# Running the F and B threads of a macro-step beside E, C, D and A, with x and h staged in one buffer each

## The chip, the cores and the metric

The kernel runs on all 8 cores of one Trainium2 chip. Each core computes one sequence of the batch and exchanges nothing with the others. The metric is the device time of the slowest core, in microseconds.

## The reference

One layer of a streaming encoder, for each sequence of 8192 frames of 1024 features:

```python
h = layer_norm(x, ln_in_g, ln_in_b)
q, k, v, g_ret, x_lru, g_lru, m_ret, m_lru = split(h @ w_in)      # 512 512 1024 1024 1024 1024 1024 1024
ret = chunk_retention(rotary(q), rotary(k), v)                    # 4 heads, 64-frame chunks, carried state
ret = head_group_norm(ret)
ret_branch = (silu(g_ret) * ret) @ w_ret_proj
hl = rg_lru(causal_depthwise_conv(x_lru))                         # gates by 8 blocks of 128x128, linear recurrence
lru_branch = (silu(g_lru) * hl) @ w_lru_proj
merged = sigmoid(m_ret + b0) * ret_branch + sigmoid(m_lru + b1) * lru_branch
h = layer_norm(2 ** 0.25 * h + merged @ w_out, ln_out_g, ln_out_b)
```

## The kernel before

**Tiling.** The 8192 frames are done in 16 macro-steps of 512 frames (TM), each in four pieces (s) of 128 frames. Weights are held in DRAM as 20 units of 128 x 4096 in bfloat16 (1 MB each; in macro-step 0 they are loaded as float32 in eight pieces of 256 KB and cast on ScalarE on the way) and go through a ring of four slots in SBUF.

**Threads.** The work of a macro-step m is written as six Python generators. Each yields after a small piece, and what it has recorded up to then goes to the in-order queues of the engines:
- A(m): for each piece, load x (512 KB), statistics, normalize (VectorE), store h to DRAM (`hscr`, issued by GpSimd), eight fp32 transposes into hT. 24 yields.
- B(m): units 0 to 3. Units 0 and 1 give q and k, with rotary on VectorE and GpSimd through the single buffers rA and rB; units 2 and 3 give v, copied by ScalarE. One PSUM bank a piece and unit. 44 yields.
- C(m): retention for two pairs of heads. For each, four recurrence steps (9 yields), then four gate groups of unit 4 or 5 (eight matmuls, four transposes, tanh, multiply; 4 yields). 104 yields.
- D(m): the gated recurrence, units 6 to 9, two channel groups in lockstep: front (two times 16 matmuls, convolution, gates) and back (root, scan, product). 13 steps a pair, 52 yields.
- E(m): units 10 to 17, for each two gates and two projections (32 matmuls) and their merge into mrg. 48 yields.
- F(m): units 18 and 19, for each piece load h from `hscr`, 16 matmuls, sum, statistics, normalize, store the output (issued by GpSimd). 16 yields.

**Order.** `interleave` takes turns: in a round each thread advances by its weight. A macro-step is two stages: first B(m+1) at weight 2 and F(m-1) at weight 1, then E(m), C(m+1) at weight 2, D(m+1) and A(m+2). There is no barrier between stages; the queues of the engines run in the order recorded. Which of the eight PSUM banks a thread may use is given by its BankPool.

**Ring.** `use(m, u)` takes a resident unit, `done(m, u)` gives its slot back and issues, on SyncE's (SP's) queue, the next unit in order of first use. All loads (units, x, h, rot) are issued by SP in the order recorded, and SP waits in that order for a tile to be free.

**Staging.** `xs` is `obuf`, two tiles of 128 x 1024: A loads x into it two pieces ahead, and F builds its output in it. `hA`, one tile, takes A's normalized h, from which it is stored and transposed, and in F the h loaded from `hscr`. A tile may be written again when its readers, a store's landing among them, are done.

## Time and profile before

| | us |
|---|---|
| median of 3 runs | 4004.73 |
| lowest and highest | 4000.53, 4128.72 |
| the profiled execution | 4020.5 |
| its slowest core (core 6), span | 4019.0 |
| its fastest core (core 3), span | 3991.4 |

The profile shows one execution, on its slowest core. TensorE's granted clock is 0.861 of full speed on that core as a mean, and 0.875 on core 3. A span runs from the first to the last instruction. Busy times of TensorE come from modelled ends, since its matmuls are pipelined.

### The profile page before, as it was taken

Reading aid. Unit: us, or ns where it says so; the run is one execution under the profiler, and the core shown is the slowest. Engines: PE = TensorE matmul, PEld = TensorE weight load, DVE = VectorE, ACT = ScalarE, POOL = GpSimd, SP = SyncE. Lnnn points to the kernel's source line nnn. Section 1 sums busy time; section 2 is a strip of 40 time slices with the busy share of each in tenths; the row PEclk is TensorE's granted clock in tenths of the full one; section 3 lists DMA queues with packets and bytes.
Section 4 is the critical chain, followed back from the end, with each engine's and each line's share of the span. In section 5 each row is a group of like instructions: output and inputs, shape, how many; then the busy total and the mean of one; then the engine's idle time right before and its main releaser. Section 6 shows DMA issues by size and latency. Waiting matters only on the chain.

```text
span 4019.0 us, 47416 instructions; the slowest of 8 cores (3991.4 to 4019.0 us)
## 1 busy us (share of the span) xinstructions
PE 2956.7 (74%) x13056; PEld 1342.7 (33%) x13056; DVE 2192.0 (55%) x3601; ACT 1608.8 (40%) x2530; POOL 1541.2 (38%) x2121
## 2 busy tenths in 40 slices
PE   0446555878787877778787877778787787878786
PEld 0222222333333333333333333333333333333332
DVE  1154333655565575665666565556656565566454
ACT  2254445242534435343434434343443534343440
POOL 0133222434353443444443443435334344434332
PEclk9766667989898998889898998889898888988888
DMA  6432433524333342424334242424334252433323
GB/s 183 143 120 81 147 118 118 181 98 168 103 133 131 108 173 87 162 105 160 111 111 156 105 163 105 170 95 145 120 114 167 89 176 95 164 116 112 122 100 142
DMA packets 109987, 522.51 MB, mean 130 GB/s; under 512 B 12448, under 2 KB 12576, under 8 KB 68768
## 3 DMA queue, kind: packets, MB, share of 16 engines
q1 hardware_dynamic: 88416, 431.38, 31.6%
q0 software_dynamic: 18432, 67.12, 4.1%
q10 hardware_dynamic: 2880, 20.97, 1.3%
q8 instruction: 111, 1.82, 0.2%
q14 instruction: 148, 1.21, 0.1%
HBM read 431.35 MB, written 88.08 MB: 129 GB/s over the span
## 4 chain that ended last, share of the span: by engine, by line
PE 38%; DVE 21%; issue 12%; ACT 10%; DMA 9%; POOL 9%; DVEq 1%; ACTq 0%; SPq 0%; POOLq 0%
PE pb L180 36%; DMA wst<-wpack 6%; DVE xc L162 5%; PE pb L184 2%; ACT ta L154 2%; DVE obuf L162 2%; POOL rA L158 2%; DVE gst L573 2%; POOL grs L158 2%; DVE S L162 1%; ACT ring L176 1%; DVE hA L162 1%; DMA obuf<-x 1%; POOL kdec L158 1%; DVE Sb L172 1%
## 5 line engine op out<-in xcount | busy, mean ns | idle before, releaser
L180 PE MATMUL pb<-hT,ring 128*128 128x512 bf16 x5120 | 1351.1, 420 | 108.0 <-DVE rA L162 87.2
L180 PEld LDWEIGHTS pb<-hT,ring 128*128 128x128 bf16 x5120 | 538.7, 106 | 774.9 <-issue 360.3
L180 PE MATMUL pb<-ring,hT 128*128 128x512 bf16 x2048 | 535.5, 420 | 158.3 <-DVE rB L158 125.1
L158 POOL TENSOR_TENSOR retT<-rB,rA 128x512 bf16<-128x512 f32 x128 | 204.7, 1600 | 489.9 <-DVE rA L162 462.5
L180 PEld LDWEIGHTS pb<-ring,hT 128*128 128x128 bf16 x2048 | 211.3, 105 | 467.1 <-issue 293.0
L154 ACT ACTIVATE xhat<-pb,gnm,grs 128x256 f32<-128x256 f32 x256 | 130.7, 561 | 585.5 <-POOL gnm L167 576.7
L180 PE MATMUL pb<-xcb,rgw_sb 128*128 128x512 bf16 x256 | 127.7, 505 | 278.7 <-DVE xcb L172 119.1
L180 PE MATMUL pb<-retT,ring 128*128 128x512 bf16 x1024 | 281.2, 424 | 63.5 <-ACT tr L154 63.1
L162 DVE SCALAR_TENSOR_TENSOR xc<-xl,vecs_sb,xc 128x512 f32<-128x512 f32 x384 | 292.0, 774 | 27.3 <-ACT xl L176 0.2
L184 PE MATMUL pb<-identf,hA 128*128 128x128 f32 x512 | 95.9, 321 | 277.5 <-DVE hA L162 150.4
L176 ACT CAST qkr<-rA 128x512 bf16<-128x512 f32 x64 | 39.6, 618 | 594.3 <-POOL rA L158 592.4
L180 PE MATMUL pb<-lruT,ring 128*128 128x512 bf16 x1024 | 243.3, 381 | 25.9 <-ACT tl L154 25.7
L672 DVE TENSOR_TENSOR_SCAN ti<-av,carry,ta 128x512 f32<-128x512 f32 x128 | 249.9, 1991 | 7.2 <-POOL ta L158 7.2
L162 DVE SCALAR_TENSOR_TENSOR rA<-rA,pb 128x512 f32<-128x512 f32 x128 | 87.8, 686 | 284.9 <-ACT rA L154 281.7
L167 POOL TENSOR_SCALAR lrs<-lmv 128x1 f32<-128x1 f32 x128 | 43.2, 338 | 518.3 <-DVE lmv L452 448.2
L180 PE MATMUL pb<-ring,mrg 128*128 128x512 bf16 x1024 | 232.7, 381 | 2.9 <-DVE rA L162 1.1
L158 POOL TENSOR_TENSOR grs<-gmv,small_sb 128x2 f32<-128x2 f32 x128 | 26.2, 204 | 514.3 <-DVE gmv L575 472.1
L158 POOL TENSOR_TENSOR mrg<-tr,tl 128x512 bf16<-128x512 f32 x128 | 163.0, 1274 | 156.2 <-DVE tl L162 154.4
L450 DVE BATCH_NORM_STATS2 lst<-obuf 128x6 f32<-128x512 f32 x64 | 44.2, 690 | 314.6 <-DMA obuf<-x 314.4
L158 DVE TENSOR_TENSOR rA<-pb,rot_sb 128x512 f32<-128x512 f32 x128 | 88.5, 692 | 210.1 <-POOL qkr L158 71.8
L154 ACT ACTIVATE rA<-pb 128x512 f32<-128x512 f32 x128 | 76.1, 595 | 309.2 <-PE pb L180 263.8
L176 ACT CAST ring<-wst 128x512 bf16<-128x512 f32 x160 | 98.8, 617 | 249.8 <-DMA wst<-wpack 202.0
(84 smaller groups left out, 5024.9 us busy)
## 6 DMA issues: line engine op xcount, KB each, us to landing
ring<-wscr SPq DMA_DIRECT2D x300, 1024.0 KB, 5.5
wst<-wpack SPq DMA_DIRECT2D x160, 256.0 KB, 3.3
obuf<-x SPq DMA_DIRECT2D x64, 512.0 KB, 5.3
hscr<-hA POOLq DMA_DIRECT2D x64, 512.0 KB, 3.5
hA<-hscr SPq DMA_DIRECT2D x64, 512.0 KB, 4.2
out<-obuf POOLq DMA_DIRECT2D x64, 512.0 KB, 3.5
wscr<-ring ACTq DMA_DIRECT2D x20, 1024.0 KB, 6.0
rot_sb<-rot SPq DMA_DIRECT2D x16, 256.0 KB, 5.8
```

The costliest lines, as they stand in the source:

```text
L154: return lambda e: e.activation(out, in_, func, **kw)
L158: return lambda e: e.tensor_tensor(out, a, b, op)
L162: return lambda e: e.scalar_tensor_tensor(out, a, sc, b, op0, op1)
L167: return lambda e: e.tensor_scalar(out, a, s1, None, op0)
L172: return lambda e: e.tensor_copy(out, in_)
L176: return lambda e: e.copy(out, in_)
L180: return lambda e: e.matmul(out, lhsT, rhs, start=start, stop=stop)
L184: return lambda e: e.transpose(out, in_, ident)
L450: S.op("dve", lambda e, xt=xt: e.bn_stats(lst[:, 0:6], xt[:, 0:512]), reads=[xk], writes=["lst0"])
L573: S.op("dve", lambda e, hl=hl, bO=bO: e.bn_stats(gs_[:, hl * 6:(hl + 1) * 6], pb[bO][:, hl * 256:(hl + 1) * 256]), reads=[PK(bO)], writes= ...
L672: S.op("dve", lambda e, c=c, di=di: e.tensor_tensor_scan(ti[di][:], av[di][:], ta[di][:], carry[:, c:c + 1], ALU.mult, ALU.add), reads=[(" ...
```

## The change

The two stages become one. In each macro-step four threads are interleaved: F(m-1) followed by E(m) (weight 1, banks 6 and 7 for both); B(m+1) followed by C(m+1) (weight 2, banks 0 and 1); D(m+1) (weight 1, banks 2 to 4); A(m+2) (weight 1, bank 5). B had banks 4 to 7 and F banks 0 to 3.

The staging becomes two tiles with one use each. `xs[0]` takes x, is normalized in place, and is stored and transposed from there. `hland[0]` takes h in F, and the sum, the normalization and the output store work in it. `load_x(m, s)` now stands right ahead of the statistics of its piece, and `load_h(m, s)` at the top of each piece of F. One tile of 128 x 1024 less is used.

```diff
--- before.py
+++ after.py
@@ -287,10 +287,8 @@
         mhalf = T("mhalf", [128, 8], F32)
         rgw = T("rgw_sb", [128, 2, 8, 128], BF16)
         ring = [T("ring%d" % i, [128, 4096], BF16) for i in range(RING)]
-        obuf = [T("obuf%d" % i, [128, D], F32) for i in range(2)]
-        xs = obuf
-        hA = [T("hA%d" % i, [128, D], F32) for i in range(1)]
-        hland = hA
+        xs = [T("xs0", [128, D], F32)]
+        hland = [T("hland0", [128, D], F32)]
         wst = [T("wst%d" % i, [128, 512], F32) for i in range(2)]
         hT = [T("hT%d" % i, [128, 8, TM], BF16) for i in range(3)]
         rot = T("rot_sb", [128, NS * 128], F32)
@@ -391,9 +389,9 @@
             S.dma("sp", "c_small", small[:], small_d, writes=["small"])
             S.dma("sp", "c_vecs", vecs[:].rearrange("p a b -> p (a b)"), vecs_d, writes=["vecs"])
             rgflat = rgw[:].rearrange("p a b c -> p (a b c)")
-            for hf in range(2):
-                S.dma("sp", "c_rgw%d" % hf, obuf[hf][:], rgw_d[:, hf * 1024:(hf + 1) * 1024], writes=[("obuf", hf)])
-                S.op("dve", f_copy(rgflat[:, hf * 1024:(hf + 1) * 1024], obuf[hf][:]), reads=[("obuf", hf)], writes=["rgw"])
+            for hf, (stg, stk) in enumerate(((xs[0], ("xs", 0)), (hland[0], ("hl", 0)))):
+                S.dma("sp", "c_rgw%d" % hf, stg[:], rgw_d[:, hf * 1024:(hf + 1) * 1024], writes=[stk])
+                S.op("dve", f_copy(rgflat[:, hf * 1024:(hf + 1) * 1024], stg[:]), reads=[stk], writes=["rgw"])
             S.op("dve", f_copy(identb[:], identf[:]), reads=["identf"], writes=["identb"])
             S.op("pool", f_memset(mhalf[:], -0.5), writes=["mhalf"])
             S.op("pool", f_memset(S32[:], 0.0), writes=[("S32", h) for h in range(4)])
@@ -424,12 +422,12 @@
                 if m >= n_macro:
                     return
                 t0 = m * TM + s * 128
-                S.dma("sp", "xl%d" % (s % 2), xs[s % 2][:], x_d[t0:t0 + 128, :], writes=[("obuf", s % 2)])
+                S.dma("sp", "xl0", xs[0][:], x_d[t0:t0 + 128, :], writes=[("xs", 0)])
 
             def load_h(m, s):
                 t0 = m * TM + s * 128
                 S.dma("sp", "hl0", hland[0][:], hscr_d[t0:t0 + 128, :],
-                      reads=[("hscr", m, s)], writes=[("hA", 0)])
+                      reads=[("hscr", m, s)], writes=[("hl", 0)])
 
 
             def hTk(m, s, half):
@@ -440,35 +438,30 @@
 
             def Athread(m, pool):
                 hTm = hT[m % 3]
-                load_x(m, 0)
-                load_x(m, 1)
+                xk = ("xs", 0)
+                xt = xs[0]
                 for s in range(NS):
-                    xk = ("obuf", s % 2)
-                    xt = xs[s % 2]
-                    hk = ("hA", 0)
-                    hb = hA[0]
-                    S.op("dve", lambda e, xt=xt: e.bn_stats(lst[:, 0:6], xt[:, 0:512]), reads=[xk], writes=["lst0"])
-                    S.op("dve", lambda e, xt=xt: e.bn_stats(lst[:, 6:12], xt[:, 512:1024]), reads=[xk], writes=["lst1"])
+                    load_x(m, s)
+                    S.op("dve", lambda e: e.bn_stats(lst[:, 0:6], xt[:, 0:512]), reads=[xk], writes=["lst0"])
+                    S.op("dve", lambda e: e.bn_stats(lst[:, 6:12], xt[:, 512:1024]), reads=[xk], writes=["lst1"])
                     S.op("dve", lambda e: e.bn_aggr(lmv[:], lst[:]), reads=["lst0", "lst1"], writes=["lmv"])
                     yield
                     S.op("pool", f_ts(lrs[:], lmv[:, 1:2], LN_EPS, None, ALU.add), reads=["lmv"], writes=["lrs"])
                     S.op("pool", f_tt(lrs[:], lrs[:], mhalf[:, 0:1], ALU.pow), reads=["lrs", "mhalf"], writes=["lrs"])
                     yield
-                    S.op("dve", f_stt(hb[:], xt[:], lmv[:, 0:1], lnig[:], ALU.subtract, ALU.mult),
-                         reads=[xk, "lmv", "lnig"], writes=[hk])
-                    S.op("dve", f_stt(hb[:], hb[:], lrs[:], lnib[:], ALU.mult, ALU.add),
-                         reads=[hk, "lrs", "lnib"], writes=[hk])
-                    if s + 2 < NS:
-                        load_x(m, s + 2)
+                    S.op("dve", f_stt(xt[:], xt[:], lmv[:, 0:1], lnig[:], ALU.subtract, ALU.mult),
+                         reads=[xk, "lmv", "lnig"], writes=[xk])
+                    S.op("dve", f_stt(xt[:], xt[:], lrs[:], lnib[:], ALU.mult, ALU.add),
+                         reads=[xk, "lrs", "lnib"], writes=[xk])
                     t0 = m * TM + s * 128
-                    S.dma("pool", "hs0", hscr_d[t0:t0 + 128, :], hb[:], reads=[hk], writes=[("hscr", m, s)])
+                    S.dma("pool", "hs0", hscr_d[t0:t0 + 128, :], xt[:], reads=[xk], writes=[("hscr", m, s)])
                     yield
                     for half in range(2):
                         b = pool.get()
                         for j in range(4):
                             kc = half * 4 + j
-                            S.op("pe", f_tr(pb[b][:, j * 128:(j + 1) * 128], hb[:, kc * 128:(kc + 1) * 128], identf[:]),
-                                 reads=[hk, "identf"], writes=[PK(b)], inc=(j == 3))
+                            S.op("pe", f_tr(pb[b][:, j * 128:(j + 1) * 128], xt[:, kc * 128:(kc + 1) * 128], identf[:]),
+                                 reads=[xk, "identf"], writes=[PK(b)], inc=(j == 3))
                         yield
                         src = pb[b][:].rearrange("p (k t) -> p k t", k=4)
                         dst = hTm[:, half * 4:half * 4 + 4, s * 128:(s + 1) * 128]
@@ -716,12 +709,10 @@
                     yield
 
             def Fthread(m, pool):
-                load_h(m, 0)
+                ob = hland[0]
+                ok = ("hl", 0)
                 for s in range(NS):
-                    ob = obuf[s % 2]
-                    ok = ("obuf", s % 2)
-                    hl = hland[0]
-                    hlk = ("hA", 0)
+                    load_h(m, s)
                     bY = [pool.get(), pool.get()]
                     for hf in range(2):
                         slot = use(m, 18 + hf)
@@ -733,13 +724,11 @@
                         done(m, 19)
                     yield
                     for hf in range(2):
-                        S.op("dve", f_stt(ob[:, hf * 512:(hf + 1) * 512], hl[:, hf * 512:(hf + 1) * 512], 2.0 * ALPHA,
+                        S.op("dve", f_stt(ob[:, hf * 512:(hf + 1) * 512], ob[:, hf * 512:(hf + 1) * 512], 2.0 * ALPHA,
                                           pb[bY[hf]][:], ALU.mult, ALU.add),
-                             reads=[hlk, PK(bY[hf])], writes=[ok])
-                    if s + 1 < NS:
-                        load_h(m, s + 1)
-                    S.op("dve", lambda e, ob=ob: e.bn_stats(lst2[:, 0:6], ob[:, 0:512]), reads=[ok], writes=["lst20"])
-                    S.op("dve", lambda e, ob=ob: e.bn_stats(lst2[:, 6:12], ob[:, 512:1024]), reads=[ok], writes=["lst21"])
+                             reads=[ok, PK(bY[hf])], writes=[ok])
+                    S.op("dve", lambda e: e.bn_stats(lst2[:, 0:6], ob[:, 0:512]), reads=[ok], writes=["lst20"])
+                    S.op("dve", lambda e: e.bn_stats(lst2[:, 6:12], ob[:, 512:1024]), reads=[ok], writes=["lst21"])
                     S.op("dve", lambda e: e.bn_aggr(lmv2[:], lst2[:]), reads=["lst20", "lst21"], writes=["lmv2"])
                     yield
                     S.op("pool", f_ts(lrs2[:], lmv2[:, 1:2], 4.0 * LN_EPS, None, ALU.add), reads=["lmv2"], writes=["lrs2"])
@@ -748,7 +737,7 @@
                     S.op("dve", f_stt(ob[:], ob[:], lmv2[:, 0:1], lnog[:], ALU.subtract, ALU.mult), reads=[ok, "lmv2", "lnog"], writes=[ok])
                     S.op("dve", f_stt(ob[:], ob[:], lrs2[:], lnob[:], ALU.mult, ALU.add), reads=[ok, "lrs2", "lnob"], writes=[ok])
                     t0 = m * TM + s * 128
-                    S.dma("pool", "os%d" % (s % 2), out_d[t0:t0 + 128, :], ob[:], reads=[ok])
+                    S.dma("pool", "os0", out_d[t0:t0 + 128, :], ob[:], reads=[ok])
                     yield
 
             def chain(*gs):
@@ -762,22 +751,21 @@
                 th.append((Athread(1, BankPool(S, [5])), 1))
             interleave(th)
             for m in range(n_macro):
-                th = []
+                p3 = BankPool(S, [6, 7])
+                g3 = [Ethread(m, p3)]
+                if m >= 1:
+                    g3.insert(0, Fthread(m - 1, p3))
+                th = [(chain(*g3), 1)]
                 if m + 1 < n_macro:
-                    th.append((Bthread(m + 1, BankPool(S, [4, 5, 6, 7])), 2))
-                if m >= 1:
-                    th.append((Fthread(m - 1, BankPool(S, [0, 1, 2, 3])), 1))
-                interleave(th)
-                th = [(Ethread(m, BankPool(S, [6, 7])), 1)]
-                if m + 1 < n_macro:
-                    th.append((Cthread(m + 1, BankPool(S, [0, 1])), 2))
+                    p1 = BankPool(S, [0, 1])
+                    th.append((chain(Bthread(m + 1, p1), Cthread(m + 1, p1)), 2))
                     th.append((Dthread(m + 1, BankPool(S, [2, 3, 4])), 1))
                 if m + 2 < n_macro:
                     th.append((Athread(m + 2, BankPool(S, [5])), 1))
                 interleave(th)
             run_gen(Fthread(n_macro - 1, BankPool(S, [0, 1, 2, 3])))
-            S.wait_all("pool", [("obuf", 0), ("obuf", 1)] + [("hscr", n_macro - 1, s) for s in range(NS)])
-            S.wait_all("sp", [("ring", i) for i in range(RING)] + [("hA", 0), "rot"])
+            S.wait_all("pool", [("hl", 0), ("xs", 0)] + [("hscr", n_macro - 1, s) for s in range(NS)])
+            S.wait_all("sp", [("ring", i) for i in range(RING)] + [("hl", 0), ("xs", 0), "rot"])
             S.wait_all("act", [("ring", i) for i in range(RING)] + [("wscr", u) for u in range(NU)])
 
         record = []
```

## Rows read from the trace of the kernel before

**Rows 1.** The page: busy time, share of the span, instructions, by engine
```profile
PE 2956.7 (74%) x13056; PEld 1342.7 (33%) x13056; DVE 2192.0 (55%) x3601; ACT 1608.8 (40%) x2530; POOL 1541.2 (38%) x2121
```

**Rows 2.** Windows: length, busy of each engine (PE, PEld, DVE, ACT, POOL), clock, DMA
```profile
1616.40:1672.60 56.20, 47.59 (x206) 20.39 (x205) 33.89 (x54) 7.78 (x14) 29.42 (x39) 0.90 0.55 195
1672.60:1717.00 44.40, 33.85 (x164) 16.40 (x162) 29.94 (x50) 21.86 (x34) 14.63 (x22) 0.85 0.48 162
1717.00:1770.40 53.40, 41.12 (x188) 19.10 (x186) 30.76 (x47) 25.29 (x40) 25.08 (x35) 0.87 0.26 96
1770.40:1809.30 38.90, 30.73 (x147) 14.01 (x145) 23.65 (x45) 18.91 (x29) 12.87 (x20) 0.87 0.24 86
1809.30:1844.50 35.20, 27.75 (x128) 13.13 (x125) 18.82 (x30) 20.59 (x32) 13.62 (x19) 0.92 0.26 90
1832.20:1844.50 12.30, 7.84 (x37) 4.19 (x36) 6.66 (x7) 8.99 (x13) 9.20 (x7) 0.92 0.27 85
3895.00:3968.00 73.00, 61.31 (x264) 26.84 (x263) 31.22 (x42) 9.63 (x14) 20.75 (x23) 0.89 0.48 173
3968.00:4019.00 51.00, 27.32 (x126) 11.97 (x123) 24.50 (x33) 2.75 (x4) 13.58 (x15) 0.81 0.28 103
```

**Rows 3.** Timeline of TensorE: start, length, instructions, idle before and releaser
```profile
1627.13 3.62 PE L180 MATMUL pb<-ring,mrg 128*128 128x512 bf16 x16
...
1630.59 3.62 PE L180 MATMUL pb<-ring,hT 128*128 128x512 bf16 x16
...
1659.11 11.66 PE L180 MATMUL pb<-ring,hT 128*128 128x512 bf16 x40 [3.38 <-DVE rB L158]
...
1841.34 2.53 PE L180 MATMUL pb<-hT,ring 128*128 128x512 bf16 x8 [2.72 <-DVE rA L162]
```

**Rows 4.** Timeline of GpSimd, at the end of the B/F stage
```profile
1655.60 1.84 POOL L158 TENSOR_TENSOR kdec<-rA,small_sb 128x512 bf16<-128x512 f32 x1
...
1665.87 0.65 POOL L108 DMA_DIRECT2D out<-obuf  x1 [1.96 <-DVE obuf L162]
```

**Rows 5.** Timeline of VectorE, the macro-step from 1616 us and the last F
```profile
1623.00 0.69 DVE L158 TENSOR_TENSOR rA<-pb,rot_sb 128x512 f32<-128x512 f32 x1 [5.61 <-DMA rot_sb<-rot]
1623.61 0.74 DVE L158 TENSOR_TENSOR rB<-pb,rot_sb 128x256 f32<-128x256 f32 x2
...
1658.88 1.48 DVE L162 SCALAR_TENSOR_TENSOR obuf<-hA,pb 128x512 f32<-128x512 f32 x2
...
1662.18 1.31 DVE L162 SCALAR_TENSOR_TENSOR obuf<-obuf,lmv,lnog 128x1024 f32<-128x1024 f32 x1
...
1678.48 0.69 DVE L450 BATCH_NORM_STATS2 lst<-obuf 128x6 f32<-128x512 f32 x1 [13.17 <-DMA obuf<-x]
...
1680.97 4.84 DVE L162 SCALAR_TENSOR_TENSOR xc<-xl,vecs_sb,xc 128x512 f32<-128x512 f32 x6
...
1711.36 4.61 DVE L672 TENSOR_TENSOR_SCAN ti<-av,carry,ta 128x512 f32<-128x512 f32 x2 [0.28 <-POOL ta L158]
...
3984.09 0.69 DVE L162 SCALAR_TENSOR_TENSOR obuf<-hA,pb 128x512 f32<-128x512 f32 x1 [2.10 <-PE pb L180]
...
4006.77 1.48 DVE L162 SCALAR_TENSOR_TENSOR obuf<-hA,pb 128x512 f32<-128x512 f32 x2
```

**Rows 6.** The page's DMA issues: count, size of one, us to landing
```profile
wst<-wpack SPq DMA_DIRECT2D x160, 256.0 KB, 3.3
...
hA<-hscr SPq DMA_DIRECT2D x64, 512.0 KB, 4.2
...
out<-obuf POOLq DMA_DIRECT2D x64, 512.0 KB, 3.5
```

**Rows 7.** Timeline of SyncE's DMA queue
```profile
1616.24 0.37 SPq L108 DMA_DIRECT2D rot_sb<-rot  x1
...
1671.33 0.81 SPq L108 DMA_DIRECT2D obuf<-x  x2
```

**Rows 8.** DMA issues of the stretch from 1640 to 1652 us
```profile
ring<-wscr SPq DMA_DIRECT2D x3, 1024.0 KB, 8.7
```

## Prediction

> **What bounds the kernel now.** I read the busy times first [rows 1]: TensorE is busy 74% of the span, VectorE 55%, nothing else over 40%. No engine is full, so the time is set by waits between engines, and a sum over engines says little. Next I looked for the period. The windows are cut where TensorE starts the first matmuls of a D unit pair or of a B stage [rows 2]: 56.2 + 44.4 + 53.4 + 38.9 + 35.2 = 228.1 us is one steady macro-step. The first window is the separate stage of B and F, the other four are the 13-round quarters of the stage of E, C, D and A. The B/F stage is already TensorE's densest (47.6 of 56.2 us); the quarters are busy 76, 77, 79 and 79%. So the stage that the change dissolves is not the one with the holes. Its own hole is B's rotary on the single rA/rB buffers: TensorE waits 3.4 us for VectorE [rows 3], which waits for GpSimd's rA and kdec work of 1.84 us [rows 4]. At its end VectorE idles 13.2 us for x [rows 5], while TensorE has forty matmuls to do, most of them of v (11.7 us, [rows 3]): that wait costs little now.
>
> **The new order, counted in rounds.** A round is one turn of the interleave. By their yields B has 44 steps at two a round (22 rounds), C 104 (52), D 52, A 24, F 16, E 48. Before, a macro-step had 22 + 52 rounds. After, F then E takes rounds 0 to 63, B then C 0 to 73, D 0 to 51, A 0 to 23. The number of rounds is 74 both times; what changes is what shares a round. Matmuls of 512 columns run at 0.216 us each at full clock (16 in 3.46 us, [rows 3]), and their number doesn't change. So the question is how long each stretch takes.
>
> **Rounds 0 to 16.** I walked the emission order with the durations of the rows. TensorE has in it 64 matmuls of F, 88 of B, 68 of D, 8 of E, and 20 transposes: about 52 us. VectorE has four F pieces at 5.7 us (two sums and the statistics from 1658.88 to about 1662, two normalizing steps of 1.3), eight rotary pieces at 1.35 (0.61 to the start of the second row, and its 0.74), three A pieces at 4.3 (statistics 1.6, normalizing 2.6), and of D two convolutions of 4.84 us, scans of 3.8 (up to 4.6) and ten smaller ones at about 0.7 (an estimate by the 0.69 of the other 128x512 rows): 67 us [rows 5]. VectorE, not TensorE, is thus the longer one here, where it was the shorter one in both stages before (33.9 of 56.2 and 29.9 of 44.4, [rows 2]). Onto it come three waits that the single buffers bring:
> - F. h, the sum and the output now share one tile. load_h(s+1) must wait until the output store has landed, then land itself. A store lands 3.5 us after its issue, a load of h takes 4.2 [rows 6], with issue about 9 us from the last multiply to the next sum; VectorE has 3 to 6 us of other work in between. Cost: 5.6 us before piece 1, 3.4 before piece 2.
> - A. The load of x stands right ahead of its statistics. For piece 1 it comes a little after h(1) and is covered. For piece 2, in round 12, it stands in SP's queue behind load_h(3) and behind three ring units (2, 10 and 3), because F has just given back two slots and B one. A 256 KB load behind one ring unit took 6.7 us (issued 1616.24, VectorE released 1623.00, [rows 5, 7]); the middle one of three ring units landed after 8.7 us [rows 8]. Three units ahead of x make some 10 us more than the 4.2 of h: 14 us, and it is VectorE that stands.
> - SP and the ring. F holds two of four slots to round 12. Unit 2, wanted in round 14, is issued behind load_h(3), that is behind the landing of out(2); TensorE waits some 10 us there, beside VectorE's wait for x and not on top of it.
> F's matmuls also have two banks instead of four and stand behind A's transposes, which wait for VectorE. The walk ends at: round 3 at 20 us, round 5 at 32, round 9 at 53, round 12 at 64, round 13 at 82, round 16 at 92 us. From below: without any DMA wait it is VectorE's 67 us plus 8 to start, 75. From above: each F piece at its full 15 us when nothing overlaps, plus the x wait, plus D's convolution behind it, 100. I take the walk's **92**.
>
> **Rounds 17 to 73.** Rounds 17 to 25 hold 100 matmuls and smalls, 25 us of TensorE work; at the 77% of the second quarter [rows 2] that is 32. Rounds 26 to 38 hold what the third quarter holds: 39. Rounds 39 to 51: like the fourth, or the second without A, so between 35.2 and 38.9: 37. Rounds 52 to 63 have E and C's recurrence without D: 18 us of TensorE work, and the third quarter scaled to 12 rounds gives 36 as the upper bound; C's serial steps fill much of it, 26. Rounds 64 to 73 are C alone, whose last four gate groups go at the pace of the present tail, 12.3 us for about three groups with TensorE waiting 2.7 us for rA in each [rows 2, 3]: four groups and the end of a recurrence step make 20. Sum 154; period 92 + 154 = 246, against 228: **+17** (rounded down for the overlap at the joint).
>
> **In place and the removed copy of the tile.** Normalizing x in x's own tile has the same instructions (1.3 us each, [rows 5]) and reads and writes no more: nothing. hscr stores and x loads stay the same in number and size.
>
> **Ends.** 13 macro-steps have all five threads: 13 x 17 = +221. In the step without A the x wait goes, the F waits stay: +10, bounds 0 and +20. The last F now runs serially: 7.0 us from its sum to the store's issue (1658.88 to 1665.87, [rows 4, 5]), 3.5, 4.2 and 0.3 make 15 a piece; now three pieces take 22.7 us (3984.09 to 4006.77, [rows 5]), 7.6 each, so +22. The same happens to F(14), and E(15) waits for its banks behind it, where now it follows at once in the 73.0 us window [rows 2]: +32. Start: up to 56 us (one B stage) can be hidden beside E(0), and each x load that falls behind a unit of eight weight loads of 3.3 us [rows 6] can stop VectorE for up to 26: 0, bounds -55 and +55. Sum on the profiled execution: 4020.5 + 221 + 10 + 22 + 32 = 4305; the median of before is 16 us under its profiled execution, so **4290** (+7%). Own bounds: period +8 to +26 with the ends, 4130 to 4430.
>
> **A page against the change.** The present kernel loads x two pieces ahead, and its only wait for x in a step is 13.2 us where the load couldn't be early [rows 5]. By that row an unprefetched load costs VectorE the load's whole time. The Trainium skill, Trainium Kernel Development and Optimization, Best Practices, says to double-buffer so that DMA overlaps compute; the change goes against it, and by the page alone it would be slower. The trace agrees where other work is short, and shows above that it costs little where TensorE has a backlog. Of stores: one lands 3.5 us after its issue in the rows. The Trainium skill, DMA: Bandwidth & Descriptors, "Anatomy of one DMA", says most of a transfer's fixed cost is the receipt of the write, which no bandwidth shortens; 2.0 us plus 524 KB at 436 GB/s would be 3.2, an estimate by that page, and the F wait would be 0.3 us shorter.
>
> **Rivals.** (a) *The waits are hidden.* If x and h land beside other VectorE work, rounds 0 to 16 take 75 us, the period is 229, and only the ends are left: 4020 + 54 - 16, about 4060. For it: VectorE has 40% of idle time over a step, and TensorE's queue may hold enough. Against it: VectorE runs in order and is the longer engine just there. 0.20. (b) *The merge fills the holes* (other side, faster). B's matmuls, wanting only banks, run in D's and C's gaps. TensorE is busy 178 to 182 us of a period (the five windows sum to 181, [rows 2]); with 30 us of waits left instead of 47, period 211: 4020 - 13 x 17 - 10 + 54 - 30 - 16, about 3800. It decides if VectorE keeps ahead of TensorE in rounds 0 to 16, i.e. if its 67 us there hide under 52 + E's work. For it: the 3.4 us rotary waits [rows 3] surely go, and the clock (0.85 to 0.92 now, [rows 2]) gains where holes close. Against it: B leaves a stage that was 85% busy, and C's tail is longer. 0.17. (c) *The queue jams*: SP's waits for landed stores hold the ring units for TensorE in each F piece, rounds 0 to 16 take over 105 us: 4450 or more. 0.06. Forecast 0.57.
>
> **How the numbers follow.** About 2% is what a measurement of this kernel can tell from no change: 3925 to 4085. Faster is (b), 0.17; same is (a) with the low end of the forecast, 0.20; slower is the rest, 0.63. The range must reach over (a) and leave out most of (b) and the top of (c): 3960 to 4430.
>
> **What would show it.** In the changed profile: no B/F stage; about 245 us from one load of rot to the next; VectorE idle until x in several places a step, the longest near the end of F, 10 us or more; VectorE idle until h of 3 to 6 us before F's sums; SP waiting for out and hscr stores; TensorE under 70% busy in the first 90 us of a step with a lower clock; gate groups of C alone at 4 to 5 us each in the last 20 us. If the period is under 229 us, the walk of rounds 0 to 16 is wrong, most likely because VectorE's load there is less tight than I count; if VectorE's waits are there but the period is short, the later rounds are.

## The result, and the profile of the changed kernel

The changed kernel takes 4411.24 us (median of 10 runs, 4397.34 to 4545.41), the kernel before 4016.14 us (10 runs, 4000.53 to 4154.93). The ratio is 1.1005, with a 95% interval of 1.0966 to 1.1045: 10% slower. In some executions of any of these kernels the cores of one die run at a lower clock and take longer; ratios leave such executions out, and two_full (all six were such) and before_banks (three of four) are read on core 2 of the profiled one, for before_banks up to 2555 us, where its clock falls. The profiled execution took 4434.0 us, with a span of 4432.4 us on core 5, 413 us more than the 4019.0 us of before.

The busy times of the page, and its chain that ended last by engine:

```profile
PE 2991.4 (67%) x13056; PEld 1362.1 (31%) x13056; DVE 2165.5 (49%) x3601; ACT 1603.9 (36%) x2530; POOL 1449.1 (33%) x2121
...
PE 35%; DVE 21%; DMA 15%; issue 11%; ACT 10%; POOL 5%; SPq 1%; DVEq 1%; ACTq 0%; POOLq 0%
```

Against [rows 1] every engine is busy for the same time within 2% (GpSimd 6% less), in a span 10% longer. Nothing was added as work; nearly all of it is waiting (TensorE's busy time grew by 35 us). In the chain DMA has 15% of the span. The chain of before had 9%.

One load of rot to the next marks a macro-step: 754.69 us, 1510.19, 1759.21, ... 4012.68 on SP's queue, 13 steps of 250.6 us. Before it was 228.7. So the steps with five threads account for 13 x 21.9 = 285 us of the 413; the start is 50 us longer (704.5 to 754.7), the step without A 24, and the end after it 54 (124 to 178).

Windows of one step of the changed kernel, cut at rounds 0, 17 (the eight matmuls of E's first unit lie at the cut), 26, 39, 52 and 64, with the columns of [rows 2]:

```profile
1509.15:1599.46 90.31, 58.31 (x235) 25.79 (x232) 55.58 (x83) 23.13 (x36) 35.57 (x53) 0.83 0.42 154
1599.46:1632.63 33.17, 29.71 (x142) 13.87 (x140) 20.90 (x29) 17.53 (x27) 9.31 (x12) 0.95 0.44 160
1632.63:1669.00 36.37, 28.93 (x138) 13.27 (x137) 21.84 (x43) 19.77 (x31) 15.46 (x27) 0.91 0.26 87
1669.00:1708.60 39.60, 33.71 (x162) 15.89 (x160) 18.30 (x31) 21.71 (x33) 12.70 (x16) 0.96 0.31 109
1708.60:1741.20 32.60, 20.73 (x102) 9.57 (x101) 14.48 (x33) 6.95 (x13) 11.44 (x19) 0.90 0.25 89
1741.20:1758.18 16.98, 10.83 (x48) 5.36 (x49) 3.50 (x8) 4.90 (x9) 5.11 (x7) 0.90 0.02 10
```

The first row is the new mixture of F, B, D and A: TensorE busy 65%, VectorE 62%, and the lowest clock of the step, 0.83. The second to fourth rows are at least as full as the quarters of before (79 to 90% busy, against 76 to 79%). In the fifth, E and C without D, TensorE is busy 64%.

The timeline of VectorE in the first row (start, length, idle before it and what ended that):

```profile
1516.53 0.69 DVE L158 TENSOR_TENSOR rA<-pb,rot_sb 128x512 f32<-128x512 f32 x1 [5.99 <-DMA rot_sb<-rot]
...
1523.69 5.59 DVE L162 SCALAR_TENSOR_TENSOR xc<-xl,vecs_sb,xc 128x512 f32<-128x512 f32 x6
...
1541.81 0.69 DVE L162 SCALAR_TENSOR_TENSOR hland<-hland,pb 128x512 f32<-128x512 f32 x1 [3.19 <-DMA hland<-hscr]
...
1558.24 0.69 DVE L158 TENSOR_TENSOR rA<-pb,rot_sb 128x512 f32<-128x512 f32 x1 [4.20 <-POOL kdec L158]
...
1579.16 0.69 DVE L158 TENSOR_TENSOR rA<-pb,rot_sb 128x512 f32<-128x512 f32 x1 [4.20 <-POOL carry L172]
...
1591.53 0.69 DVE L445 BATCH_NORM_STATS2 lst<-xs 128x6 f32<-128x512 f32 x1 [11.02 <-DMA xs<-x]
...
1616.75 0.70 DVE L445 BATCH_NORM_STATS2 lst<-xs 128x6 f32<-128x512 f32 x1 [2.72 <-DMA xs<-x]
```

Two of the on-demand loads are seen: h before F's second piece (3.2 us) and x before A's third (11.0 us). After the second and the third output store VectorE also waits 4.2 us for GpSimd before it may write rA again (the releaser is kdec the first time, carry the second). GpSimd's timeline says why:

```profile
1554.61 0.65 POOL L108 DMA_DIRECT2D out<-hland  x1 [5.15 <-DVE hland L162]
1555.28 1.60 POOL L158 TENSOR_TENSOR rA<-rA,rB 128x256 f32<-128x256 f32 x2
1557.03 1.04 POOL L158 TENSOR_TENSOR kdec<-rA,small_sb 128x512 bf16<-128x512 f32 x1
```

The output store stands in GpSimd's in-order queue ahead of B's work on rA. GpSimd idles 5.2 us until VectorE has normalized F's piece, issues the store, and only then does the work that VectorE now waits for. The third output store is issued at 1575.52 in the same way. TensorE's timeline in the same stretch:

```profile
1532.08 1.09 PE L184 MATMUL pb<-identf,xs 128*128 128x128 f32 x4 [7.22 <-DVE xs L162]
...
1563.85 1.08 PE L184 MATMUL pb<-identf,xs 128*128 128x128 f32 x4 [10.40 <-DVE xs L162]
...
1584.92 3.57 PE L180 MATMUL pb<-ring,hT 128*128 128x512 bf16 x8 [7.19 <-DMA ring<-wscr]
...
1598.99 0.63 PE L184 MATMUL pb<-identf,xs 128*128 128x128 f32 x4 [4.84 <-DVE xs L162]
```

It stands at A's transposes for VectorE's normalizing of x (7.2, 10.4 and 4.8 us), and once for a ring unit (7.2). VectorE comes late for a different reason each time: before the first of these holes ends it is at D's convolution for 5.6 us (1523.69), before the second it has idled the 4.2 us for GpSimd (1558.24), before the third the 11.0 us for x (1591.53). The matmuls after a hole run at half the clock: eight of B take 3.57 us at 1584.92, and took 1.89 at full clock. SP's queue shows where the ring unit was late:

```profile
1538.50 0.33 SPq L108 DMA_DIRECT2D hland<-hscr  x1
1540.95 0.32 SPq L108 DMA_DIRECT2D ring<-wscr  x1
1544.94 0.33 SPq L108 DMA_DIRECT2D xs<-x  x1
1557.73 21.21 SPq L108 DMA_DIRECT2D hland<-hscr  x2
1579.09 1.27 SPq L108 DMA_DIRECT2D ring<-wscr  x3
1580.46 0.45 SPq L108 DMA_DIRECT2D xs<-x  x1
```

load_h for the fourth F piece went out at the end of the merged row at 1557.73 (1557.73 + 21.21 = 1578.9), the three ring units right behind it, and x behind them at 1580.46: x landed 11 us later.

### The profile page after: what moved, and what is told of

The parts are those of the page before. It is cut to its first block, busy times and chain, and to the rows that moved or that the text cites. A ratio compares the mean times of both kernels' runs of the same rounds, so it can differ in the third digit from the quotient of the medians.

```text
span 4432.4 us, 47295 instructions; the slowest of 8 cores (4374.1 to 4432.4 us)
## 1 busy us (share of the span) xinstructions
PE 2991.4 (67%) x13056; PEld 1362.1 (31%) x13056; DVE 2165.5 (49%) x3601; ACT 1603.9 (36%) x2530; POOL 1449.1 (33%) x2121
## 4 chain that ended last, share of the span: by engine, by line
PE 35%; DVE 21%; DMA 15%; issue 11%; ACT 10%; POOL 5%; SPq 1%; DVEq 1%; ACTq 0%; POOLq 0%
PE pb L180 33%; DMA wst<-wpack 5%; DMA xs<-x 5%; DVE hland L162 4%; PE pb L184 3%; DVE xs L162 2%; DVE xc L162 2%; DMA out<-hland 2%; POOL grs L158 2%; DVE ti L665 1%; ACT ta L154 1%; ACT ring L176 1%; DMA hland<-hscr 1%; DVE gst L566 1%; ACT L154 1%
## 5 line engine op out<-in xcount | busy, mean ns | idle before, releaser
L180 PE MATMUL pb<-hT,ring 128*128 128x512 bf16 x5120 | 1299.4, 407 | 70.1 <-DVE rA L162 46.8
L184 PE MATMUL pb<-identf,xs 128*128 128x128 f32 x512 | 107.1, 349 | 582.7 <-DVE xs L162 447.4
L158 POOL TENSOR_TENSOR retT<-rB,rA 128x512 bf16<-128x512 f32 x128 | 164.6, 1286 | 515.1 <-DVE rA L162 427.4
L180 PE MATMUL pb<-ring,mrg 128*128 128x512 bf16 x1024 | 272.9, 428 | 35.9 <-DVE hland L162 35.4
L180 PE MATMUL pb<-lruT,ring 128*128 128x512 bf16 x1024 | 271.5, 413 | 5.8 <-ACT tl L154 5.8
L184 PEld LDWEIGHTS pb<-identf,xs 128*128 128x128 f32 x512 | 74.3, 178 | 629.6 <-issue 629.0
L158 DVE TENSOR_TENSOR sTm<-pb,maskT_sb 128x256 bf16<-128x256 f32 x128 | 54.2, 423 | 337.7 <-PE pb L180 337.7
L445 DVE BATCH_NORM_STATS2 lst<-xs 128x6 f32<-128x512 f32 x64 | 44.1, 689 | 349.8 <-DMA xs<-x 349.8
L176 ACT CAST qkr<-rA 128x512 bf16<-128x512 f32 x64 | 39.6, 620 | 459.0 <-POOL rA L158 457.7
L158 POOL TENSOR_TENSOR ta<-ta,ti 128x512 f32<-128x512 f32 x128 | 173.5, 1374 | 56.8 <-DVE ta L162 56.6
L180 PEld LDWEIGHTS pb<-retT,ring 128*128 128x128 bf16 x1024 | 111.3, 111 | 262.6 <-issue 196.0
```

Source lines behind the costliest of these rows:

```text
L158: return lambda e: e.tensor_tensor(out, a, b, op)
L176: return lambda e: e.copy(out, in_)
L180: return lambda e: e.matmul(out, lhsT, rhs, start=start, stop=stop)
L184: return lambda e: e.transpose(out, in_, ident)
L445: S.op("dve", lambda e: e.bn_stats(lst[:, 0:6], xt[:, 0:512]), reads=[xk], writes=["lst0"])
```

## The experiments

Twelve kernels ran, all against the kernel before on the same chip. "Front" is the time from F's first matmuls to C's first transposes (rounds 0 to 21), "back" is the rest of the step; both are read from TensorE's timeline for one step in the middle of the run, on the slowest core (core 2 for two_full and before_banks). The step is the mean of 13 (8 for before_banks) on the same core (core 2 for two_A_first, whose slowest core has 242.4). Steps of one kernel differ by some us and the cores of one execution by up to 3 us a step, so front and back don't always add up to the step: over its 13 steps the front of merged_x2f2 goes from 101.9 to 106.6 us, with a mean of 103.8, and on core 2 the steps of the kernel before and of the changed one are 228.0 and 249.5.

| kernel | front | back | step | ratio to before (95%) |
|---|---|---|---|---|
| before | 53.8 | 174.6 | 228.7 | 1 |
| changed | 115.4 | 133.7 | 250.6 | 1.1005 (1.0966 to 1.1045) |
| two_single | 60.8 | 176.4 | 240.7 | 1.0554 (1.0462 to 1.0646) |
| merged_x2 | 108.9 | 133.4 | 242.7 | 1.0671 (1.0600 to 1.0743) |
| merged_f2 | 106.4 | 133.4 | 240.5 | 1.0514 (1.0421 to 1.0606) |
| merged_x2f2 | 105.8 | 133.2 | 237.3 | 1.0382 (1.0307 to 1.0456) |
| two_full | 52.3 | 175.0 | 228.5 | none |
| full_lateA | 92.7 | 139.9 | 234.0 | 1.0268 (1.0216 to 1.0321) |
| full_lateD | 89.8 | 166.0 | 254.9 | 1.0957 (1.0894 to 1.1019) |
| after_lateA | | | 242.6 | 1.0720 (1.0683 to 1.0758) |
| before_banks | 54.9 | 176.1 | 230.9 | none |
| two_A_first | 76.1 | 166.4 | 242.6 | 1.0564 (1.0529 to 1.0598) |
| before_Dslack | 56.1 | 169.2 | 225.2 | 0.9913 (0.9878 to 0.9948) |
| full_balanced | 82.6 | 154.7 | 236.9 | 1.0405 (1.0390 to 1.0421) |

**two_single.** The changed kernel with the old order:

```diff
-                th = [(chain(*g3), 1)]
...
+                    th.append((Bthread(m + 1, BankPool(S, [4, 5, 6, 7])), 2))
+                if m >= 1:
+                    th.append((Fthread(m - 1, BankPool(S, [0, 1, 2, 3])), 1))
+                interleave(th)
+                th = [(Ethread(m, BankPool(S, [6, 7])), 1)]
```

> The old two-stage order and banks with the new staging (x and h in one buffer each, loaded on demand). Theory 1 (the on-demand, single-buffered transfers carry most of the loss): each of four F pieces needs about 15 us instead of 14, which makes the B/F stage 4 to 8 us longer, and each later x piece stops VectorE 3 to 5 us; a step of 236 to 242 us instead of 228.7, the last F some 22 us longer: 4120 to 4230 us. Rival (the merged order itself carries it: VectorE crowded beside D, thin last rounds): 4020 to 4080 us.

Measured: 4254.02 us, a step of 240.7. The single buffers alone cost 12.0 us a step and 5.5% in all, 24 us above my range. VectorE's timeline in its B/F stage shows the serial F chain that the prediction worked out:

```profile
1704.32 0.69 DVE L162 SCALAR_TENSOR_TENSOR hland<-hland,pb 128x512 f32<-128x512 f32 x1 [2.75 <-DMA hland<-hscr]
...
1720.88 0.69 DVE L162 SCALAR_TENSOR_TENSOR hland<-hland,pb 128x512 f32<-128x512 f32 x1 [6.29 <-DMA hland<-hscr]
...
1736.59 0.69 DVE L162 SCALAR_TENSOR_TENSOR hland<-hland,pb 128x512 f32<-128x512 f32 x1 [5.37 <-DMA hland<-hscr]
...
1750.29 0.69 DVE L445 BATCH_NORM_STATS2 lst<-xs 128x6 f32<-128x512 f32 x1 [6.84 <-DMA xs<-x]
```

F's pieces follow each other at 16 us, with 2.8, 6.3 and 5.4 us of waiting for h and then 6.8 for x.

**merged_x2, merged_f2, merged_x2f2.** The changed kernel with more tiles. In merged_x2 x has two, and load_x(m, s + 2) is issued at the end of piece s; in merged_f2 h has two, and load_h(m, s + 1) is issued after piece s's sum; merged_x2f2 has both (the second tile of h is that of the float32 weight pieces, free after macro-step 0).

```diff
-        xs = [T("xs0", [128, D], F32)]
+        xs = [T("xs%d" % i, [128, D], F32) for i in range(2)]
...
+                    if s + 2 < NS:
+                        load_x(m, s + 2)
...
-                    load_h(m, s)
...
+                    if s + 1 < NS:
+                        load_h(m, s + 1)
```

> The changed kernel with x in two tiles, its load emitted six rounds ahead. Theory 1: the 11.0 us wait of VectorE for x in front of the third piece goes and the smaller one of 2.7; 9 to 13 us a step come off 250.6, and some of the start: 4230 to 4300 us. Rival (the merged order): TensorE still waits for ring unit 2 behind the store of the output, and VectorE is the longer engine in rounds 0 to 16 anyway, so the wait only moves: 4360 to 4410 us.

> The changed kernel with h and the output in two tiles, h loaded a piece ahead. Theory 1: the wait of 3.2 us for h and 3 to 4 us of each step's wait for ring unit 2 and x behind the store go, and the two F runs at the end are some 22 us shorter each: 4250 to 4320 us. Rival (the merged order): only the ends, 4350 to 4380 us.

> Both together, the second tile of h being the one that the float32 weights of macro-step 0 use. Theory 1: a step of 232 to 236 us and the ends of before: 4080 to 4150 us. Rival (the merged order): a step of 242 us or more: 4230 us or more, with the time in rounds 0 to 16 where VectorE is full, and in the last 22 rounds.

Measured: 4295.11, 4272.82 and 4188.80 us. Each alone takes 7.9 and 10.1 us off a step, both together 13.3. That it is less than their sum fits that x and ring unit 2 waited behind the same load of h; no run shows it by itself. Theory 1 held for the two single changes. For both it did not: 4188.80 us lies between the two expectations, and 8.6 us a step stay that are not the transfers'. VectorE's waits for x in merged_x2f2 are the first macro-steps' only:

```profile
DVE lst L449 <- DMA xs<-x: 123.1, 4, 70.1
```

and still TensorE stands at A's transposes:

```profile
1472.59 1.09 PE L184 MATMUL pb<-identf,xs 128*128 128x128 f32 x4 [6.97 <-DVE xs L162]
...
1504.08 1.09 PE L184 MATMUL pb<-identf,xs 128*128 128x128 f32 x4 [10.18 <-DVE xs L162]
```

VectorE's and GpSimd's timelines there show what stood ahead of A's normalizing:

```profile
1464.20 5.59 DVE L162 SCALAR_TENSOR_TENSOR xc<-xl,vecs_sb,xc 128x512 f32<-128x512 f32 x6
...
1494.84 0.65 POOL L108 DMA_DIRECT2D out<-wst  x1 [8.14 <-DVE wst L162]
...
1498.47 0.69 DVE L158 TENSOR_TENSOR rA<-pb,rot_sb 128x512 f32<-128x512 f32 x1 [4.20 <-POOL kdec L158]
```

Before the first hole ends it is D's convolution. Inside the second, VectorE itself idles 4.2 us, because GpSimd has held B's work on rA behind the output store for 8.1 us: this wait is there with full staging as it is with single buffers, twice a step. The kernel before waits for GpSimd too (71.8 and 40.1 us over the run at qkr and kdec, against 61.6 and 61.5 at kdec and carry in the changed kernel), so these waits are not much more in sum; what is new is that A's normalizing, and TensorE with it, stands behind them. No run took the stores off GpSimd's queue, so what this order of the stores costs is open.

The two parts of the change are nearly additive: 12.0 for the staging in the old order, 8.6 for the merged order with full staging, 21.9 for both.

**two_full.** merged_x2f2 with the old order, as in two_single.

> The old two-stage order and banks with x in two tiles and h in two tiles, both loaded ahead. If single buffering is all that made the two-stage run of the new staging slow (240.7 us a step), this is at least as fast as the kernel before: 3960 to 4040 us. If working in place or the place of the loads costs by itself, it stays above 4100 us.

Measured: 4116.15 us. Cores 0 to 3 of the profiled execution spanned 3970.2 to 4007.4 us, against 3991.4 to 4002.4 for the same cores before. On core 2 the step is 228.5 us, before 228.0 there. So working in place costs nothing that can be told here (0.5 us a step); in this order the missing second tiles and late loads are the whole price of the staging.

**full_lateA, after_lateA.** merged_x2f2, and the changed kernel itself, with A begun 48 rounds later:

```diff
-                    th.append((Athread(m + 2, BankPool(S, [5])), 1))
+                    th.append((chain(idle(48), Athread(m + 2, BankPool(S, [5]))), 1))
```

> The merged order with two tiles each for x and h (237.3 us a step), with A started 48 rounds later, beside the thin last rounds. Theory 2 (the rest of the merge's cost is VectorE crowded by A, F, B and D in rounds 0 to 16, and a thin end): rounds 0 to 16 get some 12 us shorter and A hides where C is alone: 224 to 230 us a step, 3990 to 4080 us. Rival (the chains of C alone in the last rounds set the time, whatever lies beside them): A's four pieces lengthen these by what they take off the front, 4150 to 4210 us.

> The changed kernel as it is, single buffers and all, with A started 48 rounds later. Theory 2: the x waits now fall where VectorE has little to do, and rounds 0 to 16 are shorter: 234 to 242 us a step instead of 250.6, 4200 to 4310 us. Rival (single buffers cost the same wherever they are): 4370 us or more.

Measured: 4125.63 and 4371.72 us. The first lies between its two expectations. The front of full_lateA is 13.1 us shorter than that of merged_x2f2, as theory 2 said, but the back is 6.7 longer (11.1 and 7.6 as means of 13 steps); over 13 steps 3.3 us a step remain, on core 2 of both kernels 4.9 (237.3 to 232.4). With single buffers it is 8.0, on core 2 6.9 (249.5 to 242.6), some of it perhaps because the x waits had been on VectorE in its full stretch. By the step (242.6) theory 2 came near its upper bound; the median of 4371.72 lies over its range and would suit the rival, the ratio of 1.0720 (about 4305 us) lies at its end. In full_lateA TensorE waits now at F's own matmuls, which have two banks, until VectorE has summed the piece before (122.0 us over the run), and for A in the last rounds:

```profile
1708.52 1.86 PE L180 MATMUL pb<-ring,mrg 128*128 128x512 bf16 x4 [8.02 <-DVE hland L162]
```

```profile
1860.64 1.09 PE L184 MATMUL pb<-identf,xs 128*128 128x128 f32 x4 [4.46 <-DVE xs L162]
...
1888.96 0.63 PE L184 MATMUL pb<-identf,xs 128*128 128x128 f32 x4 [2.71 <-DVE xs L162]
```

**full_lateD.** merged_x2f2 with D begun 22 rounds later, by the same edit.

> The merged order with two tiles each, with D started 22 rounds later, so that it ends with C. Theory 2: VectorE is relieved in rounds 0 to 16 (51 instead of 67 us of its work) and C has company to the end: 222 to 230 us a step, 3960 to 4080 us. Rival (the two PSUM banks each of F and B, and the ring slots, cost the time): no better than 235 us a step, 4140 us or more.

Measured: 4406.02 us, a step of 254.9. Theory 2 fell. The front lost D's 72 matmuls and got 16 us shorter, the back took all of D and got 33 longer. Those matmuls are 15.6 us at 0.216 us each, so D had cost the front little more than its TensorE work, and it is better placed there than later. How much of the slow front is VectorE's load this run can't tell: with D VectorE's busy time went from the front too (71.1 us in merged_x2f2, 50.5 here). The front without D still has TensorE waiting:

```profile
1741.55 1.89 PE L180 MATMUL pb<-ring,hT 128*128 128x512 bf16 x8 [1.90 <-DVE rB L158]
1750.78 1.08 PE L184 MATMUL pb<-identf,xs 128*128 128x128 f32 x4 [7.34 <-DVE xs L162]
...
1776.73 1.09 PE L184 MATMUL pb<-identf,xs 128*128 128x128 f32 x4 [10.25 <-DVE xs L162]
...
1797.90 1.09 PE L184 MATMUL pb<-identf,xs 128*128 128x128 f32 x4 [5.44 <-DVE xs L162]
...
1822.62 0.39 PE L184 MATMUL pb<-identb,qkr 128*128 128x128 bf16 x4
```

22 rounds take 89.8 us for F, B, A and one unit of E, some 53 us of TensorE work. The holes at A's transposes are as long as with D there.

**before_banks.** The kernel before with the change's banks for B and F:

```diff
-                    th.append((Bthread(m + 1, BankPool(S, [4, 5, 6, 7])), 2))
+                    th.append((Bthread(m + 1, BankPool(S, [0, 1])), 2))
...
-                    th.append((Fthread(m - 1, BankPool(S, [0, 1, 2, 3])), 1))
+                    th.append((Fthread(m - 1, BankPool(S, [6, 7])), 1))
```

> The kernel before, its order and staging, with only the PSUM banks of the change: B on banks 0 and 1 instead of four, F on 6 and 7 instead of four. Theory 3 (a good part of what the merge costs is that TensorE can run only two pieces ahead of VectorE in B and F): the B/F window of 56.2 us becomes 61 to 66 us, a step 234 to 238 us, 4080 to 4150 us. Rival (the banks don't matter, the work moved beside B and F does): 4000 to 4040 us.

Measured: 4180.50 us; the shortest of its executions took 4076.62 us, between the two ranges and 1.4 to 1.9% above the 4002.35 to 4018.74 us that the kernel before took on the same chip at a like clock. On core 2 the clock is 0.88 to 0.90 to 2555 us and 0.83 and less after it; the eight steps up to there take 230.9 us each, 3.1 more than the same eight of the kernel before on core 2 (227.8), and the start is 15 us longer (692.7 to 707.8). In the old order the banks cost 3 us a step, not theory 3's 5 to 9 and not the rival's nothing. What they cost in the merged order, where F's two banks are seen to hold TensorE up in full_lateA, no run shows.

**two_A_first.** two_full with A in the first stage (banks: F 0 to 3, B 4, 6 and 7, A 5).

> Two stages, x and h in two tiles each, with A moved from the second stage to the first, beside B and F (banks: F four, B three, A one). By the run with D delayed, where A stood beside F and B too, TensorE then waits at A's transposes for VectorE. Theory 4 (moving work into the stage with rotary and F costs more there than it gives back): first stage 72 to 80 us, second 158 to 164: 232 to 240 us a step, 4060 to 4160 us. Rival (it is only two banks that made that stage slow, VectorE has room for A's 17 us): first stage 62 to 68, second 150 to 156: 214 to 222 us a step, 3820 to 3930 us.

Measured: 4232.19 us, a step of 242.6, slower even than theory 4 had it. The first stage is 24 us longer for A (76.1 us, as expected), the second 9 shorter instead of 11 to 17. TensorE's timeline in the first stage:

```profile
1704.05 3.61 PE L180 MATMUL pb<-ring,mrg 128*128 128x512 bf16 x16 [0.21 <-DVE rA L162]
...
1720.76 1.09 PE L184 MATMUL pb<-identf,xs 128*128 128x128 f32 x4 [9.64 <-DVE xs L162]
...
1742.73 1.09 PE L184 MATMUL pb<-identf,xs 128*128 128x128 f32 x4 [6.54 <-DVE xs L162]
...
1761.55 1.09 PE L184 MATMUL pb<-identf,xs 128*128 128x128 f32 x4 [5.68 <-DVE xs L162]
```

F has four banks here and B three; it is A's transposes, in TensorE's in-order queue between pieces of B and F, that wait 9.6, 6.5 and 5.7 us for A's normalizing, which stands in VectorE's in-order queue behind F's and B's work. Of the first hole VectorE itself waited 3.7 us for rot and 2.2 for x; ahead of the other two it was at work on F and B. Holes at the same place stand in the merged front (7.0 and 10.2 us in merged_x2f2, 7.3, 10.3 and 5.4 in full_lateD). Theory 4 holds, its rival (only the banks) falls.

**before_Dslack.** The kernel before with one line:

```diff
                     yield
+                    yield
                     bA = pool.get()
```

> The kernel before with one more empty round in D between the cast of xc and the block matmuls that read it, so that VectorE has a round more for the convolution: TensorE's waits for xcb and tgl (119.1 and 44.4 us in the trace of before) should shrink. If they are the bound where they stand: 3900 to 3980 us. If they only hide another wait, or D's four more rounds stand alone at the end of the stage: 4000 to 4060 us.

Measured: 3973.47 us, ratio 0.9913: the fastest of all kernels here, by less than 1%, at the upper end of the first expectation. On core 2 the step falls from 228.0 to 222.4 us (on the slowest cores from 228.7 to 225.2), while the start is 27 us longer (692.7 to 720.0). TensorE's waits there:

```profile
PE pb L180 <- ACT qkT L176: 250.2, 68, 12.1
PE pb L184 <- ACT hT L176: 199.0, 45, 20.6
```

The waits for xcb (106.5 us on this core before) are off the head of the list; in their place TensorE waits 250.2 us for qkT, which was 97.0. Most of the wait removed came back at the next dependence of the in-order queue.

**full_balanced.** merged_x2f2 with A from round 24, E ten rounds later, and D's empty round.

> The merged order with two tiles each for x and h (237.3 us a step), with three shifts at once: A begins in round 24 instead of 0, E ten rounds later so that it ends with C and not before it, and D gets the empty round that took 5.6 us a step off the kernel before. Theory 5 (a merged order is only slow where its threads crowd the front and run out at the end, and can be balanced): rounds 0 to 21 take 88 to 94 us instead of 105.8, the rest 132 to 138; 222 to 230 us a step, 3950 to 4060 us, as good as or better than the kernel before. Rival (beside B and F, whose results wait for VectorE on two banks each, other work always costs more than its own time): 233 us a step or more, 4100 us or more.

Measured: 4173.44 us, a step of 236.9. Theory 5 fell: the front became 82.6 us, even below what was expected, and the back 154.7. The wait for qkT is now

```profile
PE pb L180 <- ACT qkT L176: 354.9, 82, 36.8
```

against 231.2 in merged_x2f2. And the wait at A's transposes, 339.8 us in merged_x2f2, is here

```profile
PE pb L184 <- DVE xs L162: 143.1, 25, 94.9
```

which is no more than the kernel before has there (150.4), and still the step is 236.9. So A's transposes are where TensorE stood in the merged front, but taking that wait away didn't shorten the step: it came back at qkT, and at F's own matmuls (102.7 us).

## Why the prediction was right

The forecast was slower by 7%, 4290 us, and the kernel is slower by 10%, 4411 us; the time is in the stated range, near its top. By its steps:

- **Rounds 0 to 16.** Predicted 92 us from the walk, measured 90.3 (1509.15 to 1599.46). That the two are so close is in part luck. The waits it named are there: h before piece 1 (5.6 predicted, 3.2 measured), x before A's third piece (14, 11.0), ring unit 2 (10, 7.2). The wait of 3.4 for h before piece 2 is not: VectorE was held there by GpSimd for 4.2 us. That mechanism, an output store in GpSimd's in-order queue ahead of B's rotary work, I had not named; it takes 8.4 us here. On the other side VectorE's work in the stretch is 55.6 us and not 67, since D's second convolution (4.8 us) comes just after the cut and several terms were too large, and TensorE's is 58.3 and not 52, with the clock at 0.83. So VectorE was not the longer engine there: less work and more waiting than I had counted make nearly the same sum.
- **Rounds 17 to 73.** Predicted 32, 39, 37, 26, 20; measured 33.2, 36.4, 39.6, 32.6, 17.0. The stretch of E and C without D is the one that was mis-sized, by 6.6 us. The sum, predicted as 154, is 158.7.
- **The period.** +17 predicted, +21.9 measured as a mean of 13 steps: 4.9 x 13 = 64 of the 121 us by which the forecast is short.
- **Ends.** The last F and F(14) before E(15): +54 predicted, +54 measured. The step without A: +10 predicted, +24 measured. The start: 0 with bounds of 55 either way, +50 measured; 25 of it are there at the first load of rot (98.6 to 123.3), that is in A(0), whose pieces now load and normalize one after the other. By the third load of rot the order weighs more than the staging: that load goes out at 704.5 us in the kernel before, at 709.2 in two_single and at 740.7 in merged_x2f2. That B's stage would be hidden beside E(0) (the bound of -55) didn't come.
- **Cause.** The prediction put the loss down to VectorE being full in rounds 0 to 16 with three waits on top. The waits are shown: 13.3 of 21.9 us a step go when they are taken away. The other 8.6 come with the merged order (237.3 in merged_x2f2 against 228.7 before and 228.5 in two_full), and only their seat is in part known. TensorE stands at A's transposes in the merged front (447.4 us over the run, against 150.4 before), and A alone, moved beside B and F in the old order, costs 14 us a step (two_A_first). But A taken out of the merged front gives back only 3 to 5 of the 8.6 (full_lateA), and with the wait at its transposes gone the step is still 236.9 (full_balanced). The banks cost 3 us a step in the old order. How the 8.6 us split among A, the banks, the output stores in GpSimd's queue, which no run moved, and the back without D stays open: full_lateA and full_balanced move 13 and 23 us out of the front, and the back takes back half of the one and nearly all of the other.
- **In place.** No cost predicted, none seen (two_full).
- **Rivals.** (a), that the waits are hidden, would have left the step at 229, and it is 250.6; (b), that the merge fills the holes, is refuted with full staging too, where the step is 237.3. (c), a jam of over 105 us in rounds 0 to 16, didn't come.

## What to carry to other kernels

When every engine runs its queue in order, an interleave sets not only what can overlap but what stands in front of what: a piece whose chain goes VectorE, TensorE, ScalarE (A's normalizing and transposes) can cost far more than its work if it is put between pieces that already keep VectorE busy (14 us a step in two_A_first). A store issued by an engine that also computes holds up the work behind it until its data are ready (5.2 us of GpSimd, then 4.2 of VectorE). Look for the distance in rounds between a producer and its consumer before merging stages; one empty round in D, worth 0.9%, was the only change here that gained anything. And a load issued right ahead of its use waits not only for itself but for every wait and transfer ahead of it in the issuing queue.

## What the runs showed of the hardware

The clock falls where TensorE has its holes: in the changed kernel's first 90 us of a step it is granted at 0.83 as a mean, at 0.91 to 0.96 in the dense stretches behind them, and eight matmuls after a wait of 7.2 us take 3.57 us where they take 1.89 otherwise. The busy share alone doesn't tell it: rounds 52 to 63 are busy 64% and have 0.90, rounds 0 to 16 are busy 65% and have 0.83. Over the whole span it costs little here: the mean clock is 0.847 against 0.861 before (both on the profiled execution's slowest core), and TensorE's busy time 2991.4 us against 2956.7, 35 us of the 413.
